# The sample's part of w_b behind the prompt's part of w_out

## The reference

```python
b_out = _mla(...)                                   # attention, its last step: o @ w_b_out
x = x + (g_a * a_out + g_b * b_out) @ w_out
x = x + _expert_choice_ffn(_rmsnorm(x, norm2_g), w_router, w_gate, w_up, w_down)

aff = softmax(t @ w_router)                         # t: the normed tokens of one group
gates, idx = lax.top_k(aff.T, cap)                  # each of 16 experts picks its tokens:
xs = t[idx]                                         # 128 of the prompt, 32 of the sample
hid = silu(xs @ w_gate[e]) * (xs @ w_up[e])
y = zeros.at[idx].add((hid @ w_down[e]) * gates)
```

## Time and profile before

| what | us |
|---|---|
| median of 3 runs (2071.77 to 2073.34) | 2072.2 |
| the profiled execution | 2072.63 |
| its span | 2070.9 |
| PE busy | 2028.6 (98%) |
| PE weight loads busy | 1680.2 (81%) |
| DVE busy | 1352.0 (65%) |
| ACT busy | 952.4 (46%) |
| POOL busy | 897.6 (43%) |

### The profile page before, as it was taken

One profiled execution on the slowest core, in us unless ns is written; L12 is line 12 of the kernel. 1 busy time (PEld: TensorE's weight loads), 2 busy tenths in 40 slices (PEclk: granted clock), 3 DMA queues, 4 the chain that ended last, 5 costly groups with the idle time before them and its releaser, 6 DMA issues.

```text
span 2070.9 us, 33182 instructions
## 1 busy us (share of the span) xinstructions
PE 2028.6 (98%) x13256; PEld 1680.2 (81%) x13256; DVE 1352.0 (65%) x1608; ACT 952.4 (46%) x1181; POOL 897.6 (43%) x632
## 2 busy tenths in 40 slices
PE   8999999999999999999999999799999999999997
PEld 8888888888889888888888877677777777777775
DVE  7864455456777477777754358876777667766774
ACT  8112211113555366666630032455566555655663
POOL 0975555566655376666642601412223222222221
PEclk9999999999999999999999999999999999999999
DMA  4223444333677622231134432688887778888873
GB/s 153 105 104 134 160 161 143 129 92 129 230 253 247 216 64 87 85 102 65 57 110 158 159 143 82 242 350 317 316 302 291 279 288 317 313 316 313 303 285 107
DMA packets 168937, 398.98 MB, mean 193 GB/s; under 512 B 16512, under 2 KB 88192, under 8 KB 168832
## 3 DMA queue, kind: packets, MB, share of 16 engines
q1 hardware_dynamic: 154096, 344.43, 45.1%
q0 software_dynamic: 7680, 20.98, 4.4%
q10 hardware_dynamic: 7056, 32.12, 4.4%
HBM read 318.19 MB, written 79.30 MB: 192 GB/s over the span
## 4 chain that ended last, share of the span: by engine, by line
PE 86%; DVE 8%; ACT 2%; POOL 2%; issue 1%; DMA 1%; SPq 0%; DVEq 0%; ACTq 0%; POOLq 0%
PE PS L1697 25%; PE PS L457 13%; PE PS L458 13%; PE PS L459 13%; PE PS L1728 8%; PE PS L1481 3%; PE PS L1464 1%; PE PS L1468 1%; PE PS L1465 1%; PE PS L1466 1%; PE PS L1467 1%; PE PS L1404 1%; DVE topi L2735 1%; DVE topv L2733 1%; DVE work L2737 1%
## 5 line engine op out<-in xcount | busy, mean ns | idle before, releaser
L457 PE MATMUL PS<-act_hi,w_hi 128*128 128x256 f32 (+1 forms) x800 | 274.9, 344 | 3.7 <-DVE act_lo L2308 1.7
L458 PE MATMUL PS<-act_lo,w_hi 128*128 128x256 f32 (+1 forms) x800 | 269.7, 337 | 0.0
L459 PE MATMUL PS<-act_hi,w_lo 128*128 128x256 f32 (+1 forms) x800 | 269.3, 337 | 0.0
L1049 POOL TENSOR_SCALAR prob<-prob,small 128x1024 f32<-128x1024 f32 x64 | 185.8, 2903 | 115.2 <-DVE small L2623 115.2
L1119 POOL DMA_INDIRECT y_s<-ob_s,ixs_s x16 | 44.0, 2752 | 348.4 <-DVE ob_s L2895 348.4
L2840 DVE TENSOR_TENSOR elo<-raw,ehi 128x2048 fp32r<-128x2048 f32 x65 | 148.7, 2289 | 39.7 <-ACT ehi L2221 39.6
L457 PEld LDWEIGHTS PS<-act_hi,w_hi 128*128 128x128 f32 x800 | 151.5, 189 | 20.9 <-DVE act_lo L2308 2.1
L459 PEld LDWEIGHTS PS<-act_hi,w_lo 128*128 128x128 f32 x800 | 151.2, 189 | 16.4
L1697 PE MATMUL PS<-ehi,xT_hi 128*128 128x512 f32 x520 | 163.9, 396 | 0.6 <-DVE xT_lo L2808 0.4
L458 PEld LDWEIGHTS PS<-act_lo,w_hi 128*128 128x128 f32 x800 | 151.7, 190 | 14.7 <-issue 0.7
L1697 PE MATMUL PS<-elo,xT_hi 128*128 128x512 f32 x520 | 160.5, 390 | 0.0
(11 more groups left out here) (377 smaller groups left out, 5458.5 us busy)
## 6 DMA issues: line engine op xcount, KB each, us to landing
raw<-in_w_gate SPq DMA_DIRECT2D x64, 1024.0 KB, 8.7
raw_more<-in_w_up SPq DMA_DIRECT2D x32, 1024.0 KB, 12.6
raw_w<-in_w_up SPq DMA_DIRECT2D x32, 1024.0 KB, 16.6
w_raw<-in_w_in SPq DMA_DIRECT2D x16, 1024.0 KB, 7.7
w_raw<-in_w_down SPq DMA_DIRECT2D x15, 1024.0 KB, 6.3
stg<-in_w_down SPq DMA_DIRECT2D x15, 1024.0 KB, 8.7
gt<-in_w_down SPq DMA_DIRECT2D x15, 1024.0 KB, 13.4
raw_end<-in_w_down SPq DMA_DIRECT2D x15, 1024.0 KB, 15.3
```

The source lines that it names most:

```text
L457: pe.matmul(out, lh, rh, start=first, stop=False)
L458: pe.matmul(out, lh, rl, start=False, stop=False)
L459: return pe.matmul(out, ll, rh, start=False, stop=last)
L1049: pool.tensor_scalar(prob[:, n % 3], prob[:, n % 3], prec[:, c:c + 1], None, ALU.mult).then_inc(S["norm_pool"], 1)
```

## The change

*The attention output.* Tiles of w_b have two blocks of 512 tokens, no third. Semaphore counts follow (tile_no: two a tile from G_B on), and gates and the other branch are loaded for 0:TP alone. ACT copies the sample's part of o_hl into the sample's columns of act_hi and act_lo (late_act, behind tile 1's rounding), and the first split of wo waits for that.

*The second load.* SP loads each of the eight tiles of w_b again (load_late_w, behind the last w_out product of the prompt's chunk i), into the raw form over the columns of act_lo that this chunk leaves free; POOL splits it into the columns of act_hi and act_lo (split_late).

*The late tiles.* Behind the prompt's w_out stand eight tiles of 128 channels by 256 sample tokens (late_tile; 24 matmuls of 128x256 each) in banks 2 to 5 in turn. ACT copies a tile out (late_copy), POOL multiplies by the gate and adds the other branch (z_late), ACT rounds (late_high), POOL takes the low part (z_late_low). Each tile has landing places of its own for gate and other branch (late_in). The sample's w_out follows. Turning the lists, the chosen numbers of the first half and the flip stand between rows of the late tiles; the numbers of the second half are turned in the last half of chunk 9; keep_going is gone.

*The experts' start.* The sample's top-k stands in the first frame: lists turned after the large product l = 0, chosen numbers after 4, gathered rows after 5. few(6) of the first frame comes after l = 6. POOL takes the low parts of pieces 0, 1, 2 and 5. Pieces 0 to 2 of the first gate matrix are asked for after the last late tile, piece 3 after the gather of the prompt's rows. The normed rows of chunks 8 and 9 come from DVE, chunk 7's from POOL. ehi and elo are tensors of their own per buffer; some banks moved.

The diff, cut to its core; a line that names an engine is added to tell whose code follows:

```diff
+def tile_no(g):
+    return 3 * min(g, G_B) + 2 * max(0, g - G_B)
+def late_no(i):
+    return tile_no(G_OUT) + i + 1
...
+        def late_w(i):
+            return tuple(a[:, :, i * P:(i + 1) * P] for a in (act_hi, act_lo))
...
 SP (loads)
-                sp.dma_start(gt[:, j, :], g_d[KD + j]).then_inc(gt_in[j], 16)
+                sp.dma_start(gt[:, j, 0:TP], g_d[KD + j][:, 0:TP]).then_inc(gt_in[j], 16)
...
+            def load_late_w(i):
+                sp.wait_ge(S["out_pe"], out_no(i, 1))
+                sp.wait_ge(S["w_split"], split_no(G_END + i - 2))
+                sp.dma_start(low_raw[:, :, i * P:(i + 1) * P], w_tile("b", i)).then_inc(w_in_s[i % 2], 16)
...
-                if c == NCH - 1:
-                    sp.wait_ge(S["out_pe"], 2 * NCH)
-                    for kk in range(4):
+                if c == NCH_P - 1:
+                    load_late_w(c)
...
+                    sp.wait_ge(S["tile_pe"], late_no(KD - 1))
+                    for kk in range(3):
                         read_piece("g", 0, kk, kk)
...
 POOL
+            for i in range(KD - 1):
+                split_late(i)
+            for i in range(KD):
+                z_late(i)
+                if i > 0:
+                    z_late_low(i - 1)
+                if i == 1:
+                    split_late(KD - 1)
+            z_late_low(KD - 1)
             pool.wait_ge(S["r_in"], 48)
-            pool.wait_ge(S["r_dve"], 12)
-            for n in range(NCH_P - 1, NCH):
-                last_norm(n)
+            last_norm(NCH_P - 1)
             first_low(0)
+            first_low(1)
...
 PE
             for i in range(2, KD - 1):
                 pe.wait_ge(S["w_split"], split_no(G_B + i))
-                for b in range(3):
+                for b in range(2):
                     for k in range(KD):
                         b_block(i, b, k)
...
+            def late_tile(i):
+                hi, lo = late_w(i)
+                pe.wait_ge(S["w_split"], split_no(G_END + i))
+                if i < 4:
+                    pe.wait_ge(S["x2_dve"], out_no(6 + i // 2, i % 2))
+                else:
+                    pe.wait_ge(S["evac"], late_no(i - 4))
+                for k in range(KD):
+                    last = mm3(pe, late_bank(i), hi[:, k], lo[:, k], act_hi[:, k, TP:T], act_lo[:, k, TP:T], k == 0, k == KD - 1)
+                    if (i, k) == (0, 3):
+                        channels(NCH_P - 1)
+                    if (i, k) == (1, 0):
+                        strip_products(NCH_P - 1)
+                    if (i, k) == (1, 2):
+                        logits(NCH_P - 1)
+                    if (i, k) == (2, 2):
+                        turn_lists(1)
+                    if (i, k) == (4, 0):
+                        pe.wait_ge(S["affT_act"], 2)
+                        turn_chosen(0)
+                    if (i, k) == (5, 0):
+                        pe.wait_ge(S["chosen_act"], 1)
+                        pe.matmul(flipped_bank(), flip[:], chosen[:].rearrange("p v e -> p (v e)"), start=True,
+                                  stop=True).then_inc(S["chosen_pe"], 1)
+                last.then_inc(S["tile_pe"], 1)
...
+            for i in range(KD):
+                late_tile(i)
+            pe.wait_ge(S["evac"], late_no(KD - 1))
+            for c in range(NCH_P, NCH):
+                half_chunk(c, 0, c - 1 if c > NCH_P else None)
+                half_chunk(c, 1, None)
...
-            keep_going(20)
-            turn_chosen(1, 4)
-            keep_going(14)
-            turn_lists(2)
-            keep_going(14)
...
                     if is0 and l == 0:
-                        turn_chosen(2, 5)
-                    if is0 and l == 3:
+                        turn_lists(2)
+                    if is0 and l == 4:
+                        turn_chosen(2)
+                    if is0 and l == 5:
                         turn_xs(0)
...
-                    if l == 4 and is0:
+                    if l == 6 and is0:
                         pe.wait_ge(S["xs_dve"], 1)
                         few_product(6, lambda k: quarters(xT_s, k), 0)
...
 ACT
+                if i == 1:
+                    act.wait_ge(S["part_lo"], at("part_lo", 2 * KD))
+                    for n, a in enumerate((act_hi, act_lo)):
+                        act.activation(a[:, :, TP:T], f32(o_hl[:, :, n, TP:T]), ACT.Copy).then_inc(S["late_act"], 1)
...
+            for i in range(1, KD):
+                late_copy(i)
+                late_high(i - 1)
+                if i == 4:
+                    act.wait_ge(S["chosen_pe"], 1)
+                    act.activation(chosen[:].rearrange("p v e -> p (v e)"), chosen_bank(0), ACT.Copy)\
+                        .then_inc(S["chosen_act"], 1)
...
 DVE
-            select(1, 0, 17)
-            second_scale(8)
-            select(1, 17, 36)
-            second_scale(9)
-            select(1, 36, PICKS)
+            select(1, 0, PICKS)
             numbers(1)
...
+            for n in range(NCH_P, NCH):
+                second_norm(n)
+            first_rows_lo(0)
             affinities(2)
...
+                    if is0 and n == 4:
+                        sample_select()
+                        sample_rows()
```

More of the change, by code:

```diff
@@ L887, in _ @@
                     load_x(c + 3)
+                if c < NCH_P - 1:
+                    load_late_w(c)
+                if c == 2:
+                    for i in range(2):
+                        load_late_z(i)
+            sp.wait_ge(S["out_pe"], 2 * NCH)
+            sp.wait_ge(S["gathered_p"], 16)
+            read_piece("g", 0, 3, 3)
             def load_piece(kind, e, kk, slot):
@@ L1567, in out_product @@
             def out_product(c, h, k):
-                t = slice(c * P, (c + 1) * P)
-                last = mm3(pe, bank(out_bank(c, h)), act_hi[:, k, t], act_lo[:, k, t], wo[:, h, k, 0], wo[:, h, k, 1],
+                if c < NCH_P:
+                    hi, lo = (a[:, k, c * P:(c + 1) * P] for a in (act_hi, act_lo))
+                else:
+                    hi, lo = (z[:, c - NCH_P] for z in late_z(k))
+                last = mm3(pe, bank(out_bank(c, h)), hi, lo, wo[:, h, k, 0], wo[:, h, k, 1],
                            k == 0, k == KD - 1 and c < NCH_P)
@@ L1647, in _ @@
                         turn_lists(0)
-                    if k == 6 and (c, h) == (NCH_P, 0):
-                        turn_lists(1)
                     if c >= NCH_P and h == 1 and k in (3, KD - 1):
                         add_x(c, k // 4)
-                    if k == (1 if ready == NCH_P - 1 else 3) and ready is not None:
+                    if (c, h, k) == (NCH - 1, 1, 4):
+                        pe.wait_ge(S["x2_act"], 3)
+                        turn_chosen(1)
+                    if k == 3 and ready is not None:
@@ new lines, in _ @@
+            for c in range(HC):
+                half_chunk(c, 1, c - 1 if c else None)
+            for c in range(HC, NCH_P):
+                half_chunk(c, 0, c - 1)
+                half_chunk(c, 1, None)
+            pe.wait_ge(S["late_act"], 2)
+            for i in range(KD):
[3 more added lines that the diff above has]
+                half_chunk(c, 0, c - 1 if c > NCH_P else None)
+                half_chunk(c, 1, None)
@@ L1658, in _ @@
             channels(NCH - 1)
             strip_products(NCH - 1)
-            logits(NCH - 1)
-            turn_chosen(0, 2)
-            pe.wait_ge(S["chosen_act"], 1)
-            pe.matmul(bank(3)[:, 0:2 * E], flip[:], chosen[:].rearrange("p v e -> p (v e)"), start=True,
-                      stop=True).then_inc(S["chosen_pe"], 1)
-            def keep_going(n):
-                for _ in range(n):
-                    pe.transpose(bank(6)[:, 0:P], ident[:], ident[:])
-            keep_going(20)
@@ L2235, in frame @@
                         act.activation(xT_hi[:, KD // 2:KD], bank(3), ACT.Copy).then_inc(S["xh_act"], 1)
+                    pt = part(l, is0) if not is_last else q % 3
+                    if not (is0 and n < 2):
+                        act.wait_ge(S[f"e_in{slot}"], 16 * E + 16 if is_last else 16 * ee + 16)
+                        if not isinstance(q, int) or q >= 3:
+                            act.wait_ge(S["e_main"], q - 2)
+                        act.activation(ehi[pt][:], raws[slot], ACT.Copy).then_inc(S["e_hi"], 1)
+                    if is0 and n == 2:
+                        powers(2)
+                        list_copy(2)
                     if is1 and l == 0:
```

272 lines of the change are left out of this document (171 added, 101 removed).

## The result

The changed kernel takes 2082.9 us as the median of 4 runs (2082.49 to 2083.81), 2072.2 before; the ratio is 1.0047 with a 95% interval of 1.0035 to 1.0059. It is slower by 10.7, against a forecast of 0.7 faster and a range that ended at 2079.

The account below looks back on a forecast made before the run. PE was taken as full except a 22.1 us hand-over waiting for the top-k of the prompt's second half. Terms -22.3 + 27.1 - 16.8 + 5.8 + 3.1 + 2.4 = -0.7 took 2072.2 to 2071.5; range 2064 to 2079.

Parts of the forecast that it names:

- w_b without the sample: Attention output: 64 products of 128x256 at 0.36 go from PE, a gain of 22.3.
- from there to the end of w_out, with clock: Late tiles: 23.0 of products, a 4.5 wait in tile 5, 0.7 evacuation, less 1.1, plus 1.6 of clock.
- end of w_out to the gathered rows: Hand-over to the experts: only POOL's gather is left, 5.3 in place of 22.1, a gain of 16.8.
- first expert without the wait behind it, with clock: First expert: PE waits of 1.5, 2.2 and 3.6 for the sample's top-k and rows; 5.8 lost, plus 0.8 of clock.
- second expert: wait, and all behind it: Second expert: reload and low part 1.9 late, DVE 1.2 late by the fourth product; 3.1 lost, nothing later.
- T in the prediction: Time of the end of the prompt's last w_out product: 1266.9 before, then 22.3 earlier.
- The cover for the top-k: Late tiles and sample's w_out: second top-k runs T+10 to T+46, turned at T+55, 9 to spare; failing 0.03.
- The clock as a whole: Half clock behind PE's waits: 1.6 at tile 5, 0.8 in the first expert, 2.4 together; bounds 0 and 4.8.
- Tile 5's wait: Late tile 5: PE waits 4.5 for ACT's copy; rival says the wait is absent, 2065.4, chance 0.27.
- the gathers: First expert: rival says both gathers land late behind other DMA traffic, adding 6.8, 2078.3, chance 0.15.
- POOL's splits: Prompt's w_out: rival says second w_b splits slow DVE's norms and top-k, 1.3 per norm, 2075.4, chance 0.07.
- three signs of being wrong: PE waits for POOL's low parts; tile 5's wait is under 1 or over 8; the experts' period changes.

Follow-up runs that it names:

- e1_fill: The changed kernel with transposes of the identity that nobody reads put ahead of each PE wait: 2075.3 us, ratio 1.0014 to the kernel before.
- e4_nokeep: The kernel before with its 48 transposes of the identity left out, nothing else: 2072.9 us, ratio 1.0000.
- e3_low2: The changed kernel with the low part of the first gate matrix's piece 2 on DVE, not POOL: 2077.5 us, ratio 1.0024 to the kernel before.
- f2_fillX: The changed kernel with 4, 9 and 8 transposes of the identity around the end of w_out alone: 2082.8 us.
- f3_fillE2: The changed kernel with 23 transposes of the identity ahead of the second expert's first product alone: 2080.9 us.
- f4_ix: The changed kernel with DVE's low part of piece 6 held until POOL has copied the sample's index: 2080.9 us.
- e2_flip7: The changed kernel with only the flip product and ACT's copy of it moved from late tile 5 to late tile 7: 2076.5 us.
- g1_early: The changed kernel with flip in tile 7, piece 2 on DVE, index wait, fillers, earlier sample top-k, POOL taking piece 4 not 5: 2066.7 us.

## Why the prediction was wrong, point by point

The measured column is taken from the two profiled runs.

| step | forecast | measured |
|---|---|---|
| w_b without the sample, to chunk 7's transposes | -22.3 | -21.9 |
| from there to the end of w_out, with clock | +28.7 | +30.4 |
| end of w_out to the gathered rows | -16.8 | -16.4 |
| first expert without the wait behind it, with clock | +6.6 | +12.8 |
| second expert: wait, and all behind it | +3.1 | +5.1 |
| sum | -0.7 | +9.9 |

The medians lie 10.7 apart, 11.4 over the forecast. Of that the clock has some 7.8 by the count (10.2 on the path against 2.4) and the late lists 2.1.

*w_b.* Right. Of the 0.4 nothing is shown: PE waits 1.41 for chunk 7, before 1.02, but in the variants, whose code is the same up to there, this wait is 0.80 to 2.32 and the place itself lies between 1245.9 and 1248.9. T in the prediction stands 1.2 behind the true end of the prompt's last product; it is the same on both sides and drops out.

*The late tiles.* The tiles, the wait of 4.25 and its chain (table load, POOL's sums, tile 7's split between) came as worked out. The copy came at 1266.52. The clock behind it cost 3.1, not 1.6.

*The cover for the top-k, the gap after w_out.* Right: DVE was done with the second list at 1291.6, 11.5 before PE asked. The rows were turned 6.8 behind the last residual add, before 23.2.

*The first expert.* This step failed, in two terms. The clock: 0.8 forecast for all waits of the first expert, 4.2 measured on the path (1.7 in the second product, 2.5 after the sample's rows) beside 1.7 hidden. And the lists: forecast at 6.2 after the turned rows, measured at 8.3, because POOL's low part of piece 2 blocked DVE's 0.2 step for 2.4. I had costed the work that moved to POOL at its own duration and nothing for what it does to DVE. The gather itself was faster than I took it (2.8 from issue to landing, where the earlier trace rows had 4.5 as the least), which took back 1.7 of the 2.1 that the blocked copy cost. The trace of the kernel before had the sign: POOL's copy of the sample's index takes 0.18 in the first expert, and 2.17 in the second, where it lies beside DVE's low part (1340.33 to 1342.62).

```profile
1328.84 0.18 POOL L1104 COPY ixg_s<-rows 128x1 uint32<-128x1 uint32 x1 [11.73 <-DVE gates L2829]
...
1340.49 2.17 POOL L1104 COPY ixg_s<-rows 128x1 uint32<-128x1 uint32 x1
```

*The second expert.* The wait was 3.0, forecast 3.1, with both its parts, but in another place: elo came 1.8 late, and DVE's xT_lo (1.22) stood behind it and ahead of PE's first product, where the forecast had a second wait at the fourth. Its half clock, 3.0 by the count and 2.7 by the rows, was not in the sum at all.

*The clock as a whole.* This is the term that was mis-sized: 2.4 forecast, with 4.8 as the upper bound; 10.2 on the path by the count, of which e1_fill gave back 9.4 in its profile, and the upper bound was wrong too. Three faults went into it. I took one recovery of 3 us as the size, where the stretches measured last 3.5 to 7.5. The kernel before already had two stretches and not one: its clock is back at 1.00 behind the first 20 transposes, and the wait of 3.88 for the chosen numbers brings it down again.

```profile
1310.50:1311.00 0.50, 0.00 (x0) 1.00 0.99 393
...
1313.50:1314.00 0.50, 0.17 (x2) 0.50 0.00 0
```

I charged 0.8 for all the waits of the first expert and nothing for the second's, where four of the five waits of 2.3 to 4.3 in the changed kernel brought half clock. And I took the fillers, which were being removed, for work that computes nothing, so costs nothing to lose: in the kernel before they were not needed (e4_nokeep), because the long wait stood ahead of work that had slack; the change spread the waiting over six places in dense work, and all but one of the low stretches fell where there was no slack. The rule of the Trainium skill that I weighed against the row ("TensorE: Matmul & The Clock Gate", section "HAM oscillation — how this bites in real kernels") was nearer than the row I went by, and would still have been short, since I allowed it three places.

*The rivals and the signs.* No rival was the case. Tile 5's wait was there, the gathers were not late, and chunk 7's transposes came within 0.4 of the forecast, so POOL's splits cost DVE's norms nothing that shows. POOL and DVE did collide, but in the first expert. None of the three signs of being wrong came either (tile 5's wait was 4.25, PE never waited for POOL's low parts, the experts' period stayed the same): they looked at waits alone, and the loss lay in how fast PE works behind them.

*Slips without weight.* keep_going is 9.3 of the 12.4 that PE is busy in the hand-over, not nearly all of it. The experts' period is 45.9 in both kernels; 46.9 is the length of the window that was asked for. 9.0 less 7.2 is 1.8.

That the clock is the main cause is shown by e1_fill, in which nothing but idle transposes is added and 7.6 of the 10.7 go, and by the second expert, which takes 2.7 less in the runs where its clock stays up behind the same wait; the port is shown by e3_low2. Not settled is why a given wait brings half clock in one run and none in another, or a short stretch in one and a long one in the next.

## What to carry to other kernels

Where a change splits one long wait of TensorE into several short ones inside dense work, price each of them with the half clock behind it (here about 1.5 or about 2.7 us a time, as the second expert shows it), and ask for each whether PE is what the next step waits for; where it has slack the loss is free. Cure the waits by the order first: here the order without any filler gave 12.0 us, and fillers behind it 2.2, within the noise. Where a wait stays, fillers ahead of it that last as long as it does (here 0.12 us each) held the clock up: alone they gave 7.6. Work moved to GpSimd is to be priced twice, by its own time and by each DVE step with two inputs in SBUF that falls beside it; and a copy or a gather's issue on GpSimd waits in turn for such a DVE step. And a result that is copied early is not free if an in-order engine has to wait for it: ask for it where it is used.

## What was not expected of the hardware

Behind the waits in dense work the half clock stretches came in two lengths, 3.5 to 4 us (1.4 to 1.7 lost by the count) and 7 to 7.5 (2.5 to 3.1 lost), and the same code gave either: behind the same wait of 4.25 in late tile 5 the changed kernel lost 3.1, f2_fillX 2.8, f3_fillE2 3.1, but e3_low2 and f4_ix 1.7. The window of f4_ix:

```profile
1267.50:1271.50 4.00, 3.59 (x17) 0.57 0.02 4
1271.50:1275.00 3.50, 3.50 (x31) 1.00 0.00 0
```

Nor does the length of a wait decide whether it comes. In the changed kernel the wait of 2.34 at the lists brought it and that of 2.29 at the chosen numbers did not; in e2_flip7 a wait of 3.40 at the lists brought none and one of 2.31 behind it did. Ahead of the second expert 3.00 brought a long stretch in the changed kernel, 2.95 a short one in f2_fillX, and 3.18 and 3.02 none in e3_low2 and f4_ix. With waits of at most 1.8 and fillers between, in g1_early, there was none. An indirect DMA's issue on POOL goes from 1.01 to 2.48 beside a DVE operation with two inputs in SBUF (f4_ix), and to 2.24 at the second expert's gather in the same two kernels; the max and find steps of the top-k, with one input, ran beside POOL's 4.5 us low part at their usual 0.4 to 0.5.
